# A ring of three 48 KB thirds for the expert weights, and pooling matrices loaded packed

## What is computed

```python
n = rms_norm(h, norm1_w)
q, k, v, u = split(n @ w_in)                       # 512, 128, 128, 512 columns
a = sliding_window_attention(q, k, v, sinks)       # window 128, rotary, QK norm
p = multiscale_pool(u, pool_w, pool_scale)         # causal means over 2/4/8/16 tokens, minus u, times pool_w
h = h + concat(a, p) @ w_out
x = rms_norm(h, norm2_w)
for each token, for its 4 of 32 experts e with gate weight g:
    gu = x @ w_gu[e] + b_gu[e]                     # w_gu[e]: 1024 x 2048, 8 MB
    gate, up = min(gu[:1024], 7), clip(gu[1024:], -7, 7)
    y += g * ((gate * sigmoid(1.702 * gate) * (up + 1)) @ w_down[e] + b_down[e])   # 1024 x 1024, 4 MB
out = h + y
```

## Time and profile before

| | |
|---|---|
| median of 3 runs | 988.81 us (988.5 to 988.91) |
| the profiled execution's own time | 988.7 us |
| its span, first to last instruction | 986.9 us |
| TensorE busy (x4508) | 946.6 us, 96% |
| VectorE, ScalarE, GpSimd busy | 202.9, 127.7, 14.0 us |
| mean granted TensorE clock | 0.987 |
| DMA, whole span | 418.27 MB, mean 424 GB/s |

### The profile page before, as it was taken

One profiled execution on the slowest core, in us unless ns is written; L12 is line 12 of the kernel. 1 busy time (PEld: TensorE's weight loads), 2 busy tenths in 40 slices (PEclk: granted clock), 3 DMA queues, 4 the chain that ended last, 5 costly groups with the idle time before them and its releaser, 6 DMA issues.

```text
span 986.9 us, 11112 instructions
## 1 busy us (share of the span) xinstructions
PE 946.6 (96%) x4508; PEld 382.4 (39%) x4508; DVE 202.9 (21%) x610; ACT 127.7 (13%) x346; POOL 14.0 (1%) x9
## 2 busy tenths in 40 slices
PE   9999999999999899898989989889989999999997
PEld 5545433333333334333333333333333333333432
DVE  4645121212111121210112121011212112111121
ACT  2433111011110111010011101001101110011101
POOL 0031000000000000000000000000000000000000
PEclk9999999999999999999999999999999999999999
DMA  9999999999999999999999999999999999999996
GB/s 374 426 423 398 412 429 434 432 430 428 432 431 429 436 430 430 434 432 429 434 433 426 437 432 428 437 430 429 436 429 431 432 429 430 431 433 430 422 422 272
DMA packets 23869, 418.27 MB, mean 424 GB/s; under 512 B 2912, under 2 KB 3296, under 8 KB 8224
## 3 DMA queue, kind: packets, MB, share of 16 engines
q1 hardware_dynamic: 23408, 417.20, 99.2%
q10 hardware_dynamic: 432, 0.66, 0.2%
HBM read 416.80 MB, written 1.05 MB: 423 GB/s over the span
## 4 chain that ended last, share of the span: by engine, by line
PE 63%; DMA 36%; DVE 1%; issue 0%; ACT 0%; SPq 0%; DVEq 0%
DMA ring<-w_gu_dram 33%; PE ps L1237 29%; PE ps L1342 14%; PE ps L1205 4%; PE ps L1189 4%; DMA ring<-w_down_dram 3%; PE ps L1066 3%; PE ps L997 2%; PE ps L1004 1%; PE ps L1293 1%; PE ps L1301 1%; PE ps L1013 0%; PE ps L1039 0%; PE ps L1058 0%; PE ps L1046 0%
## 5 line engine op out<-in xcount | busy, mean ns | idle before, releaser
L1237 PE MATMUL ps<-ring,passing 128*64 128x512 f32 x1008 | 229.1, 604 | 14.8 <-DMA ring<-w_gu_dram 14.8
L1237 PE MATMUL ps<-ring,PR 128*64 128x512 f32 x976 | 224.5, 608 | 16.4 <-DMA ring<-w_gu_dram 16.2
L1342 PE MATMUL ps<-ring,PT 128*64 128x512 f32 x984 | 218.3, 595 | 0.5 <-DMA ring<-w_down_dram 0.5
L952 DVE TENSOR_SCALAR xw<-ps 128x256 f32<-128x256 f32 x64 | 27.2, 425 | 650.0 <-PE ps L1237 650.0
L1237 PEld LDWEIGHTS ps<-ring,passing 128*64 128x64 f32 x1008 | 76.8, 139 | 158.3 <-issue 143.8
L1237 PEld LDWEIGHTS ps<-ring,PR 128*64 128x64 f32 x976 | 74.9, 140 | 157.0 <-issue 145.4
L1342 PEld LDWEIGHTS ps<-ring,PT 128*64 128x64 f32 x984 | 68.1, 137 | 129.6 <-issue 127.5
L652 ACT ACTIVATE xw<-xw 128x256 f32<-128x256 f32 x64 | 26.6, 416 | 484.5 <-DVE xw L952 484.5
L1205 PE MATMUL ps<-PT 64*128 64x512 f32 x248 | 69.7, 640 | 0.0
L1189 PEld LDWEIGHTS ps<-qk,X 128*128 128x128 f32 x512 | 59.6, 191 | 18.8 <-issue 18.8
L1189 PE MATMUL ps<-qk,X 128*128 128x128 f32 x512 | 65.7, 281 | 0.0
(11 more groups left out here) (198 smaller groups left out, 374.6 us busy)
## 6 DMA issues: line engine op xcount, KB each, us to landing
ring<-w_gu_dram SPq DMA_DIRECT2D x48, 4096.0 KB, 28.2
ring<-w_down_dram SPq DMA_DIRECT2D x25, 4096.0 KB, 29.7
ring<-w_gu_dram SPq DMA_DIRECT2D x14, 2048.0 KB, 14.2
ring<-w_gu_dram SPq DMA_DIRECT2D x6, 3072.0 KB, 23.2
ring<-w_down_dram SPq DMA_DIRECT2D x5, 2048.0 KB, 23.1
ring<-w_gu_dram SPq DMA_DIRECT2D x9, 1024.0 KB, 9.6
ring<-w_down_dram SPq DMA_DIRECT2D x8, 1024.0 KB, 25.9
ring<-w_down_dram SPq DMA_DIRECT2D x2, 3584.0 KB, 27.6
```

The source lines that it names most:

```text
L952: nc.vector.tensor_scalar(gb[:, b, :], gu[:, b, 0, :], LIMIT, None, ALU.min).then_inc(g_ready, 1)
L1237: last = mm(ps[64 * j:64 * j + 64, GU + b, :], lhs, halves[j][:, 512 * b:512 * b + 512], start=start, stop=stop)
L1342: last = mm(ps[64 * j:64 * j + 64, bank, :], at[:, k, 64 * (c - GU_PIECES):64 * (c - GU_PIECES) + 64], rows[:, 512 * j:512 * j + 512], sta ...
```

## The change

The ring has nine slots (144 KB a partition), used as three thirds. w_gu and w_down become one array `w_all`, in which an expert is two rows of 48 KB a partition: an even third with gate/up pieces 0 to 2, and an odd one with gate/up piece 3 and both down pieces. From the seventh third on SP loads one third, 6 MB, by one transfer, as soon as all three pieces of its place are free; TensorE waits before gate/up pieces 0 and 3 alone. The four `extra` blocks go; piece 8 is loaded in their place. Ahead are now the first gate/up chunk of experts 26 to 29 and a second block of expert 26 (`later_ahead`), 5 MB. `END_CUTS` stay like before, with (30, 0) listed as one cut, and the last down chunk comes as two transfers of 256 of its 512 columns each half, multiplied, copied out and added to the tokens half by half. TensorE runs experts 2 to 25 in a loop of two rounds of twelve, and the b_down matmuls stand behind that loop, before expert 26. The pooling matrices are stored as 1,408 bytes a partition (bf16 for the exact part, float32 for the first 16 columns), and four GpSimd copies write the float32 matrices of 4,352 bytes; the pooling matmuls wait for those, the following product for `pool_w`.

```diff
--- before.py
+++ after.py
+EDGE = max(POOLS)
+PACKED = NG * (P + EDGE) // 2 + NG * EDGE
 NE, TOPK, FF = 32, 4, 1024
 LIMIT, ALPHA = 7.0, 1.702
 EPS, QK_EPS = 1e-5, 1e-6
@@ -53,24 +55,30 @@
 PASSES = SEQ // SLOTS
 PIECES = 6
 GU_PIECES = 4
-RING = 8
+RING = 9
 TURN = 4
 TURNS = NE // TURN
 TP = TURN * PIECES
-LAST_TWO = [(2, c) for c in range(GU_PIECES)] + [(3, c) for c in range(GU_PIECES)] + [(u, c) for u in (2, 3) for c in range(GU_PIECES, PIECES)]
 PIECE = 4096
-PAIR = 2 * PIECE
-FIRST_FILL = (1, 2, 2, 3)
-BY_CHUNK, SINGLES = (RING, RING + 1, RING + 3), 14
-MORE_LANDINGS, LATER_LANDINGS = (3, 1, 3, 1), (1, 1, 1, 0)
-END_CUTS = {(2, 2): ((4, 6), (6, 8)), (3, 0): ((0, 2), (2, 4)), (3, 2): ((4, 6), (6, 7), (7, 8)),
-            (2, 4): ((0, 2), (2, 4), (4, 6), (6, 7), (7, 8)), (3, 4): ((0, 2), (2, 4), (4, 6), (6, 7), (7, 8))}
+PART = 3
+TRIPLE = PART * PIECE
+SLOTS_OF = RING // PART
+HALVES = NE * 2
+FIRST_PLACE = (NE - 2) * PIECES
+LAST_TWO = [(e, c) for e in (NE - 2, NE - 1) for c in range(GU_PIECES)] + [(e, c) for e in (NE - 2, NE - 1) for c in range(GU_PIECES, PIECES)]
+BY_CHUNK, SINGLES = (RING, RING + 1, RING + 3), 12
+LANDINGS = (2, 3, 4, 4, 6, 3, 3)
+END_CUTS = {(NE - 2, 0): ((0, 4),), (NE - 2, 2): ((4, 6), (6, 8)), (NE - 1, 0): ((0, 2), (2, 4)), (NE - 1, 2): ((4, 6), (6, 7), (7, 8)),
+            (NE - 2, 4): ((0, 2), (2, 4), (4, 6), (6, 7), (7, 8)), (NE - 1, 4): ((0, 2), (2, 4), (4, 6), (6, 7))}
+LAST_COLUMNS = ((0, 256), (256, 512))
 X_CUTS, W_CUTS = ((0, 1), (1, 2), (2, 4), (4, 8)), ((0, 1), (1, 2), (2, 3), (3, 4), (4, 6), (6, 8))
 H_CUTS = (((0, 512), (512, 1024)), ((0, 512), (512, 896), (896, 1024)))
 ROUNDS = 3
 NR = NE * (PASSES + 1)
 
-AHEAD = 6
+AHEAD = 4
+AHEAD_FROM = NE - 2 - AHEAD
+ROUND_PARTS, ROUND_EXPERTS = 12, 12
...
-        "w_gu": w_gu.reshape(NE, 2, 4, P, 2, 2, 2, FF // 4).transpose(0, 1, 3, 2, 5, 6, 4, 7).reshape(NE * 2, P, PAIR),
-        "w_down": w_down.reshape(NE, 8, P, DM).transpose(0, 2, 1, 3).reshape(NE, P, PAIR),
+        "w_all": np.concatenate([w_gu.reshape(NE, 8, P, 2, 2, 2, FF // 4).transpose(0, 2, 1, 4, 5, 3, 6).reshape(NE, P, GU_PIECES * PIECE),
+                                 w_down.reshape(NE, 8, P, DM).transpose(0, 2, 1, 3).reshape(NE, P, (PIECES - GU_PIECES) * PIECE)],
+                                2).reshape(NE, P, 2, TRIPLE).transpose(0, 2, 1, 3).reshape(HALVES, P, TRIPLE),
...
-        extra = sb("extra", [P, 4, 1024])
...
+        packed = front[:, KC * INW + NG * (REACH + 2 * P):KC * INW + NG * (REACH + 2 * P) + PACKED]
+        exact = packed[:, 0:NG * (P + EDGE) // 2].bitcast(BF16).rearrange("p (g s) -> p g s", g=NG)
+        edge = packed[:, NG * (P + EDGE) // 2:PACKED].rearrange("p (g s) -> p g s", g=NG)
...
-            *(extra[:, n, :] for n in range(4)))]
...
-        down_ahead = [mixP[:, :, :].rearrange("p g s -> p (g s)"), xT[:, FF:2 * FF]]
+        later_ahead = [mixP[:, :, :].rearrange("p g s -> p (g s)"), xT[:, FF:2 * FF]]
...
-            sp.dma_start(band, bands.rearrange("p (g s) -> p g s", g=NG)).then_inc(ld_bands, 16)
-            sp.dma_start(poolw, w_pool.rearrange("p (g n) -> p g n", g=NG)).then_inc(ld_bands, 16)
+            sp.dma_start(packed, bands).then_inc(ld_bands, 16)
+            sp.dma_start(poolw, w_pool.rearrange("p (g n) -> p g n", g=NG)).then_inc(ld_poolw, 16)
...
+            def load(part, slot, first=0, stop=TRIPLE, at=None):
+                at = slot * TRIPLE + first if at is None else at
+                dst = ring[:, at:at + stop - first].rearrange("p (o n) -> p o n", o=1)
+                return sp.dma_start(dst, w_k[:, bass.ds(part, 1), first:stop])
 
             def load_piece(s, first=0, stop=PIECE):
 
-                e, c = s // PIECES, s % PIECES
-                src, row = (w_dn_k, e) if c >= GU_PIECES else (w_gu_k, e * 2 + c // 2)
-                load(s % RING, row, src, first, stop).then_inc(landed[s % RING // 2], 16)
-            def load_pair(s, first=0, skip=0):
-                slot, e, c = s % RING, first + s // PIECES, s % PIECES
-                src, row = (w_gu_k, e * 2 + c // 2) if c < GU_PIECES else (w_dn_k, e)
-                load(slot, row, src, skip, PAIR).then_inc(landed[slot // 2], 16)
+                part, base = s // PART, s % PART * PIECE
+                load(part, part % SLOTS_OF, base + first, base + stop).then_inc(landed[part % SLOTS_OF], 16)
+            def load_part(part, skip=0, rounds=0):
+                slot = part % SLOTS_OF
+                load(rounds + part, slot, skip).then_inc(landed[slot], 16)
...
+                sp.dma_start(later_ahead[j], w_k[:, 2 * AHEAD_FROM + 1, j * FF:(j + 1) * FF]).then_inc(ld_later_ahead[j], 16)
...
-            load_pair(0)
+            load_piece(0, stop=2 * PIECE)
             load_piece(RING + 2)
-            for n in range(8, 2 * AHEAD):
-                load_ahead(n)
+            load_piece(RING - 1)
             sp.wait_ge(proj, 2)
             load_piece(3)
...
-            for s in range(RING + SINGLES, RING + 2 + TP, 2):
-                sp.wait_ge(pieces_used, s + 2 - RING)
-                load_pair(s)
-            with sp.Fori(1, TURNS - 3) as r:
-                for s in range(RING + 2, RING + 2 + TP, 2):
-                    sp.wait_ge(pieces_used, r * TP + s + 2 - RING)
-                    load_pair(s, r * TURN)
-            for s in range(RING + 2, 3 * TP - 2 * PIECES, 2):
-                sp.wait_ge(pieces_used, (TURNS - 3) * TP + s + 2 - RING)
-                gu_ahead = 0 <= s - TP < AHEAD * PIECES and s % PIECES == 0
-                load_pair(s, NE - 3 * TURN, 2 * FF if gu_ahead else DM if s in (TP + GU_PIECES, TP + PIECES + GU_PIECES) else 0)
+            first_part = (RING + SINGLES) // PART
+            with sp.Fori(0, 3) as r:
+                for part in range(first_part, first_part + ROUND_PARTS):
+                    sp.wait_ge(pieces_used, r * (PART * ROUND_PARTS) + PART * (part + 1) - RING)
+                    load_part(part, rounds=r * ROUND_PARTS)
+            for part in range(first_part + 3 * ROUND_PARTS, HALVES - 4):
+                sp.wait_ge(pieces_used, PART * (part + 1) - RING)
+                begun = part >= 2 * AHEAD_FROM and (part % 2 == 0 or part == 2 * AHEAD_FROM + 1)
+                load_part(part, 2 * FF if begun else 0)
             for n in range(0, 2 * PIECES, 2):
-                u, c = LAST_TWO[n]
-                s = 3 * TP - 2 * PIECES + n
-                sp.wait_ge(pieces_used, (TURNS - 3) * TP + s + 2 - RING)
-                slot, ex, down = s % RING, NE - TURN + u, c >= GU_PIECES
-                src, row, wide = (w_dn_k, ex, DM) if down else (w_gu_k, ex * 2 + c // 2, 2 * FF)
-                if (u, c) in END_CUTS:
-                    for k, stop in END_CUTS[u, c]:
-                        base = PAIR if c == 2 else 0
-                        load(slot, row, src, k * wide - base, stop * wide - base).then_inc(landed_end[u, c, k], 16)
-                else:
-                    load(slot, row, src, 0, PAIR).then_inc(landed[slot // 2], 16)
+                e, first_c = LAST_TWO[n]
+                sp.wait_ge(pieces_used, FIRST_PLACE + n + 2 - RING)
+                per, wide = (4, DM) if first_c >= GU_PIECES else (2, 2 * FF)
+                def place_of(k):
+                    c = k // per + (GU_PIECES if first_c >= GU_PIECES else 0)
+                    slot = (FIRST_PLACE + LAST_TWO.index((e, c))) % RING
+                    return 2 * e + c // PART, c % PART * PIECE + k % per * wide, slot * PIECE + k % per * wide
+                for k, stop in END_CUTS[e, first_c]:
+                    part, first, at = place_of(k)
+                    load(part, 0, first, first + (stop - k) * wide, at).then_inc(landed_end[e, first_c, k], 16)
+                if (e, first_c) == (NE - 1, GU_PIECES):
+                    part, first, at = place_of(KC - 1)
+                    ends = ring[:, at:at + DM].rearrange("p (j n) -> p j n", j=2)
+                    rows = w_k[:, part, first:first + DM].rearrange("p (j n) -> p j n", j=2)
+                    for q, (a, b) in enumerate(LAST_COLUMNS):
+                        sp.dma_start(ends[:, :, a:b], rows[:, :, a:b]).then_inc(landed_cols[q], 16)
...
+            pool.wait_ge(ld_bands, 16)
+            for dst, src in ((band[:, :, EDGE:REACH], exact[:, :, 0:P]), (band[:, :, REACH + EDGE:REACH + P], exact[:, :, 0:P - EDGE]),
+                             (band[:, :, REACH:REACH + EDGE], exact[:, :, P:P + EDGE]), (band[:, :, 0:EDGE], edge)):
+                nc.gpsimd.tensor_copy(dst, src).then_inc(unpacked, 1)
...
-            down_out(NE - 1, 0, GU + 1, ye_last)
+            act.wait_ge(pieces_used, NE * PIECES)
+            for done, (a, b) in zip((y_first, y_sb), LAST_COLUMNS):
+                nc.scalar.copy(ye_last[:, a:b], ps[:, GU + 1, a:b]).then_inc(done, 1)
...
-            pe.wait_ge(ld_bands, 32)
+            pe.wait_ge(unpacked, 4)
...
```

(73 more changed lines are left out.)

97 lines of the change are left out of this document (36 added, 61 removed).

## The result

The changed kernel takes 1001.02 us (median of 4 runs, 1000.6 to 1001.69) against 988.86 us in 4 runs of the kernel before made beside them: 1.012 times, with an interval of 1.0108 to 1.0132, so 12.2 us slower. The profiled execution took 1000.7 us, its span is 998.8. The forecast was 993.5.

What follows compares the result with a forecast made beforehand. The weight stream was taken to bound the kernel. Bytes -0.9, transfers -2.8, hand-over +2.1, end +5.5 and clock +0.8 summed to +4.7 us on a median of 988.81: 993.5 us, range 986.5 to 996.5.

Steps and rivals of the forecast that it cites:

- The end: From expert 25's odd third on: TensorE alone sets the end, 6.6 us behind the last byte instead of 1.1, +5.5 us.
- The hand-over: Where loads pass from pieces to thirds, near 155 to 171 us: the queue runs dry once, +2.1 us.
- some 0.85 us: Hand-over step: time from an issue to moving data, read from the store issued at 982.13.
- even without a gap at its start: Hand-over step: first third, issued at 155.1 against a queue through at 155.3, given no gap; queue dry at 169.8.
- Transfers: Weight queue: 30 fewer transfers at about 0.10 us each, 3.0 us, less 0.2 for the halves' 1 KB runs: -2.8 us.
- rows of 48 KB: Thirds' transfers: taken at the 32 KB rows' rate; rival, up to 0.1 us dearer per third, 5.3 us, 998.8, chance 0.08.
- Bytes: Weight queue: pooling matrices shrink from 544 KB to 176 KB, 0.38 MB less, -0.9 us.
- Clock: TensorE's tail: a slower clock after expert 25's wait adds 1.7 us or none; +0.8 us taken.
- GpSimd and the columns: Front and last row: GpSimd copies, about 1.0 us, done by 25, cost 0; column halves and early copy gain 0.

Runs made afterwards that it cites:

- a_singles: Changed kernel with pieces 21 to 26 still loaded one by one, so whole thirds begin at the tenth: 998.91 us, 1.0101.
- b_unrolled: Kernel before with only TensorE's experts 4 to 23 written out instead of run as a four-expert loop: 992.06 us, 1.0029.
- a_six: Changed kernel without expert 26's second block loaded ahead, its room a third token buffer, loop of six experts: 998.1 us (1001.61 without buffer and shorter loop).
- b_bands: Kernel before with the packed pooling matrices and GpSimd's four copies alone: 989.52 us, 1.0006.
- a_bdn: Changed kernel with the eight b_down matmuls back behind expert 1, ahead of the loop: 1003.28 us, 1.0146.
- h_split: Changed kernel with its first two whole thirds (pieces 21 to 26) as three 2 MB transfers each, issued at the same counts: 1001.04 us, 1.0121.
- a_six_all: a_all with the third token buffer and TensorE's loop of six experts: 994.13 us, 1.0051.
- h_split_all: a_six_all with its first two 6 MB transfers (pieces 27 to 32) as three of 2 MB each, at the same counts: 993.84 us, 1.0052.
- a_all: Changed kernel with pieces 21 to 26 single, b_down behind expert 1, odd thirds of experts 25 to 29 in two transfers: 995.74 us, 1.0068.

## Why the prediction was wrong

**The end: right.** From expert 25's odd third TensorE takes 820.41 to 991.13, 170.7 us against the 170.4 worked out, b_down at 836.62 included, with no DMA wait behind the 0.9 us for that third itself. The lag came out at 5.2 instead of 6.6 us because the stream lost time behind 820 too.

**The hand-over: right in kind, too small.** The forecast had one dry place and 2.1 us; it was two and 5.3. Two steps failed. One is "some 0.85 us" from issue to data, read off the start of a store's packets. The weights' first packet starts much like it, 1.0 us after the issue (156.41), but the sixteen engines start spread over another microsecond, and each one's first packet of 48 KB takes 1.9 to 3.0 us where later ones take 1.8; by their completions they start 2 to 2.8 us after the issue. The other is that the first third was given no gap ("even without a gap at its start"). By the forecast's own numbers, an issue at 155.1 and a queue through at 155.3, it had 0.2 us to cover 0.85; measured were 1.1 us (155.43 against a landing at 156.5), and that is too short by far. Pieces issued one by one remove both gaps (a_singles). The Trainium skill (DMA: Bandwidth & Descriptors, Specifications) gives some 0.6 us to the first byte; the trace doesn't agree on a queue that has just run dry, where the first packet starts after 1.0 us and the engines are 2 us behind the issue.

**A term was missing: TensorE's code.** This is the step that cost most. The diff makes the loop of four experts one of twelve, and the forecast's sum has no term for instructions at all: it put their cost at nothing without a reason. The Trainium skill (Runtime: NRT & Kernel Launch, Instruction fetch mechanics) gives TensorE's instruction memory 128 KiB, refilled by 16 KiB. An expert's code is about 16 x 29.06 / 25.7 = 18 KB, an estimate from one 16 KB fetch every 25.7 us in after, two of them at the loop's end; b_unrolled, with 17 fetches in 490 us and no loop, gives 16. So six are 97 to 109 KB and eight 130 to 145. The runs agree: six stay and eight don't. The Trainium skill calls the cost of crossing a block mostly hidden; here, where DMA is the bound, it isn't. A fetch's packet takes about 1.04 us, and by the sixteen completions in the trace it moves one of the engines that carry the weights back by some 1.55 us, which it keeps through the steady part. The spread between the first and the last engine for one transfer stays near 2.45 us from 290 to 780 us before; after it grows from 2.4 to 7.0, and the transfer is there only when the last engine is. In the chain these are the three distances of 59.7 us, 4.6 us by expert 25. b_unrolled and a_six show 3.0 and 3.5 us.

**Smaller terms.** Transfers: two of 6 MB take 29.06 us and three of 4 MB 29.14 (9.713 each, the mean of the landings' distances before), so one more costs 0.08 us and 30 fewer gave some 2.3 us of the 3.0; rows of 48 KB cost nothing extra that shows, and that rival falls. Bytes: -0.9 us didn't show (b_bands), and at 156.5 us the stream is where it was before instead of 1.2 ahead. Clock: expert 25's wait was 0.9 us and the clock stayed at 1.00, so 0 instead of 0.8; a_bdn and h_split show the other case. GpSimd and the columns: nothing, as predicted; the four copies take 1.5 us instead of 1.0 and are done by 25.1, as these lines show.

```profile
23.57 1.30 POOL L537 CAST ring<-ring 128x512 f32<-128x512 bf16 x3 [23.12 <-DMA ring<-bands_dram]
24.81 0.24 POOL L537 COPY ring<-ring 128x64 f32<-128x64 f32 x1
```

**The sum.** The time is the landing of expert 25's third plus TensorE's tail. The forecast's own terms put that landing at 812.9: a span of 986.9 + 4.7 = 991.6, less the 7.5 behind the down product, the tail of 170.4 and the 0.8 of clock. It came at 820.4, 7.5 later, which adds up to within 0.1: 1.2 for the front, 3.2 for the hand-over (5.3 - 2.1), 4.6 for the fetches, and 1.6 back, as 43 thirds took 43 x 14.53 = 624.8 us where the forecast leaves 812.9 - 186.5 = 626.4. With 0.3 more for the tail, 0.2 for what follows it and 0.8 less for the clock these are the 7.2 us between 993.5 and the profiled 1000.7.

**Still open.** Why a_six_all and h_split_all stay 5 us over the kernel before is explained in part only. Their landings show 3.5 to 4.2 us lost at their own hand-over and 1.5 by a late fetch, against some 2 us that fewer transfers bring; and up to 3 us come or go around 115 to 130 us, where several of the variants have landings 1 to 2.8 us late in their profiled executions. In the three with the latest (a_singles, a_all, b_bands) TensorE also begins its first expert 0.8 to 1.3 us later than in after; what sets that is not shown. No version tried beats the kernel before.

## What to carry to other kernels

When a change lengthens a loop's body, count its instructions per engine: past what stays resident, every round is fetched again by the same DMA engines that carry the data, and a stream that is the bound pays (3.0 to 3.5 us in 990 here). Look for the instruction queue's packets in a stretch of steady work; there should be none, as in the kernel before. And a coarser transfer has to be issued some 4 to 5 us before the one in front of it lands, and it moves the end of the kernel by what the compute engine must still do after its last landing. When two kernels take equal times, compare their landings and the clock before calling them alike (h_split).

## What the runs showed that was not expected

- The delays by fetches don't average out. With 19 fetches in 490 us, each on one engine, the mean rate in that stretch is 432 GB/s as before; only the spread between the engines grows, and landings follow the slowest. Nor do the fetches fall on all engines alike: in the transfer that lands at 292.6 eight of the sixteen completions lie within 0.4 us of the earliest and eight 1.5 to 2.4 us behind it; at 791.4 seven still lie within 0.4 us and one at 1.6, and the other eight are 4.5 to 7.1 us behind. So the 20 fetches in between fall on about half of the engines, and the last landing jumps three times by 1.5 us, which are the 4.6 us.
- The end of a loop round costs TensorE an idle time of its own when the body isn't resident: 2.85 us in after. The DMA waits behind it take it up: TensorE has none for the third that lands at 499.1, where two experts earlier it waited 1.1 us and one earlier 2.6, and 0.9 at the next (528.2). b_unrolled and a_six have none of it (0.2 us at most).

```profile
489.06 3.41 PE L1256 MATMUL ps<-ring,passing 128*64 128x512 f32 x8 [2.85 <-issue]
```

- How much queue is needed. By the landings, a 6 MB transfer issued with 1.1 us of work in front of it lost 3.1 us, with 2.8 lost 2.2, with 3.5 lost 2.1 (a_six_all, issue 199.62), with 3.8 lost 0.6 (a_singles, issue 198.36) and with 5.3 lost nothing (its issue at 182.43). The order is plainer by the earliest of the sixteen completions: from the issue to the moment from which that engine works at full pace again are 1.8 to 2.0 us in five of six such places (the first in after and in a_bdn, both in a_six_all, 198.36 in a_singles; 2.6 for the second in after), and the last engine is another 1.5 to 3 us behind the first.
